# Two-part fp32 products: the high weights meet both halves of the operand in one 512-column matmul, in the FFN output and the last MLP

## The reference, cut to what matters

```
def swiglu(n, w_ffn_in, w_ffn_out):            # first block; its output projection is touched
    g, u = jnp.split(n @ w_ffn_in, 2, axis=-1)
    return (jax.nn.silu(g) * u) @ w_ffn_out     # 2816 -> 1024

def sq_relu_mlp(x, w_up, w_down):               # second block, layer 1 of 2 (the last MLP) is touched
    hdn = jax.nn.relu(x @ w_up)                 # 1024 -> 4096
    return (hdn * hdn) @ w_down                 # 4096 -> 1024

h = h + sq_relu_mlp(rms_norm(h, norm_mlp[i]), mlp_w_up[i], mlp_w_down[i])
```

## Time and profile before

| what | value |
|---|---|
| time, 3 runs | 1304.88, 1305.71, 1305.90 us; median 1305.71 |
| the profiled execution's own time | 1304.97 us |
| its span, first to last instruction | 1303.2 us (mean granted TensorE clock 0.985) |
| busy in the span | PE 1244.8 us (96%), DVE 862.6 us (66%), ACT 672.1 us (52%), POOL 36.5 us (3%) |
| chain that ended last | PE 85%, DVE 10%, ACT 3% of the span |

### The profile page before, as it was taken

The page is one execution under the profiler, slowest core; times in us unless marked ns, Lnnn a source line. Parts: engine busy times, 40 slices in busy tenths (PEclk is TensorE's granted clock), DMA queues, the critical chain, the costliest instruction groups (busy, mean ns, idle before and its releaser), DMA issues.

```text
span 1303.2 us, 26044 instructions
## 1 busy us (share of the span) xinstructions
PE 1244.8 (96%) x9778; PEld 1199.2 (92%) x9778; DVE 862.6 (66%) x1308; ACT 672.1 (52%) x1027; POOL 36.5 (3%) x58
## 2 busy tenths in 40 slices
PE   5989999999998999999799999999999988999997
PEld 5989779999997999999799879999999977999996
DVE  6897674888755877765754545766554869766543
ACT  6443435657444656644434454655444685666331
POOL 1001220200000000000100000000000000000000
PEclk9999999999999999999899999999999988999999
DMA  5455333475552566565354202555555435556651
GB/s 198 138 162 162 114 97 114 130 236 185 163 161 97 172 187 189 179 191 181 103 187 127 68 1 85 169 170 174 179 177 172 150 111 154 179 188 182 188 179 65
DMA packets 56759, 197.52 MB, mean 152 GB/s; under 512 B 7136, under 2 KB 9440, under 8 KB 56560
## 3 DMA queue, kind: packets, MB, share of 16 engines
q1 hardware_dynamic: 54144, 194.01, 48.0%
q10 hardware_dynamic: 2544, 2.51, 0.6%
HBM read 195.45 MB, written 1.05 MB: 151 GB/s over the span
## 4 chain that ended last, share of the span: by engine, by line
PE 85%; DVE 10%; ACT 3%; issue 2%; DMA 1%; SPq 0%; DVEq 0%; ACTq 0%
PE acc L392 23%; PE acc L394 23%; PE acc L393 23%; DVE wlo L1246 3%; PE acc L437 2%; PE acc L438 2%; PE acc L439 2%; ACT whi L863 1%; PE mix L521 1%; DVE xc L1450 1%; PE mix L734 1%; DVE uu L1735 1%; DMA raw<-w 1%; PE mix L695 1%; PE mix L744 1%
## 5 line engine op out<-in xcount | busy, mean ns | idle before, releaser
L863 ACT ACTIVATE whi<-raw 128x1024 fp32r<-128x1024 f32 x368 | 388.1, 1058 | 464.4 <-PE acc L394 405.4
L1246 DVE TENSOR_TENSOR wlo<-raw,whi 128x1024 fp32r<-128x1024 f32 x368 | 449.5, 1223 | 220.9 <-ACT whi L863 220.4
L392 PE MATMUL acc<-xh,whi 128*128 128x256 f32 (+1 forms) x1664 | 479.1, 288 | 24.0 <-DVE xl L1253 20.7
L394 PE MATMUL acc<-xh,wlo 128*128 128x256 f32 (+1 forms) x1664 | 474.7, 285 | 0.0
L393 PE MATMUL acc<-xl,whi 128*128 128x256 f32 (+1 forms) x1664 | 474.5, 285 | 0.0
L392 PEld LDWEIGHTS acc<-xh,whi 128*128 128x128 f32 x1664 | 317.4, 191 | 29.5 <-DVE wlo L1246 17.6
L394 PEld LDWEIGHTS acc<-xh,wlo 128*128 128x128 f32 x1664 | 318.0, 191 | 0.0
L393 PEld LDWEIGHTS acc<-xl,whi 128*128 128x128 f32 x1664 | 316.5, 190 | 0.2
L393 PE MATMUL acc<-hl,whi 128*128 128x256 f32 (+1 forms) x688 | 195.4, 284 | 0.0
L392 PE MATMUL acc<-hh,whi 128*128 128x256 f32 (+1 forms) x688 | 195.0, 283 | 0.0
L394 PE MATMUL acc<-hh,wlo 128*128 128x256 f32 (+1 forms) x688 | 194.7, 283 | 0.0
(11 more groups left out here) (322 smaller groups left out, 1478.3 us busy)
## 6 DMA issues: line engine op xcount, KB each, us to landing
raw<-w SPq DMA_DIRECT2D x368, 512.0 KB, 3.6
hT<-xT ACTq DMA_DIRECT2D x1, 1024.0 KB, 10.4
mem<-memT ACTq DMA_DIRECT2D x1, 1024.0 KB, 6.0
out<-hT SPq DMA_DIRECT2D x8, 128.0 KB, 2.0
xdt<-wsmall ACTq DMA_DIRECT2D x1, 192.0 KB, 10.2
pr<-par ACTq DMA_DIRECT2D x1, 114.0 KB, 10.1
hT<-metaT ACTq DMA_DIRECT2D x1, 64.0 KB, 11.5
bcn<-wa ACTq DMA_DIRECT2D x1, 32.0 KB, 10.1
```

The costliest lines, as they stand in the source:

```text
L392: nc.tensor.matmul(dst, whi[:, slot, n, :], rh, start=first, stop=False)
L394: return nc.tensor.matmul(dst, wlo[:, slot, n, :], rh, start=False, stop=last)
L863: act.activation(whi[:, j, :, :].rearrange("p k c -> p (k c)"), raw[:, j, :], ACT.Copy)\
L1246: dve.tensor_tensor(wlo[:, j, :, :].rearrange("p k c -> p (k c)"), raw[:, j, :], whi[:, j, :, :].rearrange("p k c -> p (k c)").bitcast(F32 ...
```

## The change

All three passes stay in the arithmetic, but the two that share `whi` become one instruction. The operand's high and low parts now lie side by side in one tile (`xboth`, `hboth`), and `wide` issues one matmul of 2 x 256 columns with `whi`, whose first half goes to columns 0 to 255 of the bank and whose second half to columns 256 to 511, and one of 256 columns with `wlo`, into the first half. The two halves of the bank are added up when the bank is read out. This is done for the 256-token phases `ffo`, `up1` and `dn1`; all other phases keep `products`.

```
-        xh = sb("xh", [P, KB, T2], F32R)
-        xl = sb("xl", [P, KB, T2], F32R)
+        xboth = sb("xboth", [P, KB, 2, T2], F32R)
+        xh, xl = xboth[:, :, 0, :], xboth[:, :, 1, :]
...
+        hboth = sb("hboth", [P, MLP_KB, 2, T2], F32R, stack=s3)
+        low = sb("low", [P, 4, T1], stack=s3)
+        hh, hl = hboth[:, :, 0, :], hboth[:, :, 1, :]
... TensorE
+            def wide(bank, slot, n, r, first, last):
+                nc.tensor.matmul(acc[:, bank, :].rearrange("p (a t) -> p a t", a=2), whi[:, slot, n, :], r, start=first,
+                                 stop=False, skip_group_check=True)
+                return nc.tensor.matmul(acc[:, bank, 0:T1], wlo[:, slot, n, :], r[:, 0, :], start=False, stop=last,
+                                        skip_group_check=True)
... ffo, DVE
-                    dve.tensor_tensor(h, acc[:, m % 4, 0:T1], h, ALU.add).then_inc(evacuated[m % 4], 1)
+                    dve.tensor_tensor(h, acc[:, m % 4, 0:T1], h, ALU.add).then_inc(joined, 1)
+                    dve.wait_ge(joined, m + 1)
+                    dve.tensor_tensor(h, acc[:, m % 4, T1:2 * T1], h, ALU.add).then_inc(evacuated[m % 4], 1)
```

```
+            def relu_squared(i, j):                                    # ACT, body of units_loop("up1")
+                act.wait_ge(unit_done, 4 * i + (UNITS["up1"][0] + j + 1))
+                act.activation(low[:, j, :], acc[:, j, T1:2 * T1], ACT.Copy).then_inc(low_ready, 1)
+                act.wait_ge(hid_ready, 4 * i + (2 * FFN_KB + MLP_KB + j + 1))
+                act.activation(blk(hh, 4 * i + j, 0, T1), t4[:, j, 0:T1], ACT.Copy).then_inc(hh_ready, 1)
... DVE, after inverse_rms("mlp1", T1)
-            units_loop("up1", *mlp_up(1, T1))
+            dve.tensor_tensor(rstdh[:, 0:T1], rstd[:, 0:T1], rstd[:, 0:T1], ALU.mult).then_inc(rstdh_ready, 1)
+            dve.wait_ge(rstdh_ready, 2)
+            def hid_sum(i, j):                                         # before split_lo of the unit four ahead
+                t = t4[:, j, 0:T1]
+                dve.wait_ge(low_ready, 4 * i + j + 1)
+                dve.wait_ge(hl_ready, 4 * i + (FFN_KB + MLP_KB + j - 3))
+                dve.tensor_tensor(t, acc[:, j, 0:T1], low[:, j, :], ALU.add).then_inc(evacuated[j], 1)
+            def hid_square(i, j):                                      # after it
+                t = t4[:, j, 0:T1]
+                dve.wait_ge(evacuated[j], i + (OUTS["up1"] // 4 + 1))
+                dve.scalar_tensor_tensor(out=t, in0=t, scalar=0.0, in1=t, op0=ALU.max, op1=ALU.mult)\
+                    .then_inc(hid_ready, 1)
+            units_loop("up1", hid_sum, hid_square)
... dn1, DVE, for each of 8 outputs
-                        dve.tensor_tensor(h, acc[:, m % 4, 0:T1], h, ALU.add).then_inc(evacuated[m % 4], 1)
+                        dve.tensor_tensor(t, acc[:, m % 4, 0:T1], rstdh[:, 0:T1], ALU.mult).then_inc(scaled_done, 1)
+                        dve.tensor_tensor(v, acc[:, m % 4, T1:2 * T1], rstdh[:, 0:T1], ALU.mult)\
+                            .then_inc(evacuated[m % 4], 1)
+                        dve.wait_ge(scaled_done, 2 * m + 1)
+                        dve.tensor_tensor(h, t, h, ALU.add).then_inc(scaled_done, 1)
+                        dve.wait_ge(evacuated[m % 4], (OUTS["dn1"] + m) // 4 + 1)
+                        dve.wait_ge(scaled_done, 2 * m + 2)
+                        dve.tensor_tensor(h, v, h, ALU.add).then_inc(joined, 1)
... POOL
+            with pool.Fori(0, MLP_KB // 4) as i:
+                for j in range(4):
+                    b = 4 * i + j
+                    pool.wait_ge(hh_ready, 4 * i + (FFN_KB + MLP_KB + j + 1))
+                    pool.tensor_tensor(blk(hl, b, 0, T1), t4[:, j, 0:T1], blk(hh, b, 0, T1).bitcast(F32), ALU.subtract)\
+                        .then_inc(hl_ready, 1)
```

More of the change, by code:

```diff
@@ L230, in blocks_kernel @@
         s3 = ExitStack()
-        hh = sb("hh", [P, MLP_KB, T2], F32R, stack=s3)
-        hl = sb("hl", [P, MLP_KB, T2], F32R, stack=s3)
+        hboth = sb("hboth", [P, MLP_KB, 2, T2], F32R, stack=s3)
+        low = sb("low", [P, 4, T1], stack=s3)
+        hh, hl = hboth[:, :, 0, :], hboth[:, :, 1, :]
         s3.close()
@@ L287, in blocks_kernel @@
         sm_step, pv_done = sem("sm_step"), sem("pv_done")
+        low_ready, sum_done, scaled_done = sem("low_ready"), sem("sum_done"), sem("scaled_done")
+        joined = sem("joined")
         hid_ready, hh_ready, hl_ready = sem("hid_ready"), sem("hh_ready"), sem("hl_ready")
@@ L394, in products, with wide_unit @@
                 return nc.tensor.matmul(dst, wlo[:, slot, n, :], rh, start=False, stop=last)
+            def wide(bank, slot, n, r, first, last):
[3 more added lines that the diff above has]
+                                        skip_group_check=True)
+            def wide_unit(phase, m, j, turn=None, ready=None):
+                u0, e0 = UNITS[phase][0], OUTS[phase]
+                pe.wait_ge(lo_ready, m + (u0 + 1))
+                pe.wait_ge(evacuated[j], (e0 + m) // 4 if turn is None else turn + e0 // 4)
+                for k in range(KB):
+                    if ready is not None:
+                        pe.wait_ge(ready[0], ready[1] + k + 1)
+                    last = wide(j, (u0 + j) % 4, k, xboth[:, k, :, 0:T1], k == 0, k == KB - 1)
+                last.then_inc(unit_done, 1)
             def unit(phase, m, j, ah, al, T, turn=None, ready=None):
@@ L710, in ffn_down @@
                         pe.wait_ge(hl_ready, k + 1)
-                    last = products(acc[:, m % 4, 0:T1], (u0 + b // 8) % 4, b % 8, hh[:, k, 0:T1], hl[:, k, 0:T1],
-                                    k == 0, k == FFN_KB - 1)
+                    last = wide(m % 4, (u0 + b // 8) % 4, b % 8, hboth[:, k, :, 0:T1], k == 0, k == FFN_KB - 1)
                     if b % 8 == 7:
@@ L787, in mlp @@
             def mlp(n, T):
-                project(f"up{n}", xh, xl, T, operand(f"mlp{n}"),
-                        statistics=lambda: stream_stats(f"mlp{n}", T))
+                if T == T1:
+                    for j in range(4):
+                        wide_unit(f"up{n}", j, j, ready=operand(f"mlp{n}") if j == 0 else None)
+                        if j == 0:
+                            stream_stats(f"mlp{n}", T)
+                    with pe.Fori(1, MLP_KB // 4) as i:
+                        for j in range(4):
+                            wide_unit(f"up{n}", 4 * i + j, j, turn=i)
+                else:
+                    project(f"up{n}", xh, xl, T, operand(f"mlp{n}"),
+                            statistics=lambda: stream_stats(f"mlp{n}", T))
                 with pe.Fori(0, 2) as i:
@@ L803, in deep4 @@
                         pe.wait_ge(hl_ready, hid0 + k + 1)
-                    last = products(acc[:, m, 0:T], (u0 + k // 8) % 4, k % 8, hh[:, k, 0:T], hl[:, k, 0:T],
-                                    k == 0, k == MLP_KB - 1)
+                    if T == T1:
+                        last = wide(m, (u0 + k // 8) % 4, k % 8, hboth[:, k, :, 0:T1], k == 0, k == MLP_KB - 1)
+                    else:
+                        last = products(acc[:, m, 0:T], (u0 + k // 8) % 4, k % 8, hh[:, k, 0:T], hl[:, k, 0:T],
+                                        k == 0, k == MLP_KB - 1)
                     if k % 8 == 7:
@@ L1229, in _ @@
             rms("mlp1", T1, (), 8)
-            units_loop("up1", mlp_up(1, T1))
+            def relu_squared(i, j):
[3 more added lines that the diff above has]
+                act.activation(blk(hh, 4 * i + j, 0, T1), t4[:, j, 0:T1], ACT.Copy).then_inc(hh_ready, 1)
+            units_loop("up1", relu_squared)
             u0 = UNITS["dn1"][0]
@@ L1235, in _ @@
                         split_hi(u0 + 4 * m + n + 4)
-                act.wait_ge(evacuated[m % 4], (OUTS["dn1"] + m) // 4 + 1)
+                act.wait_ge(joined, KB + m + 1)
                 square(m, T1)
@@ L1843, in _ @@
                     if n == 3:
-                        h = hT[:, m, META:T2]
-                        dve.tensor_tensor(h, acc[:, m % 4, 0:T1], h, ALU.add).then_inc(evacuated[m % 4], 1)
+                        h, t, v = hT[:, m, META:T2], t4[:, m % 4, 0:T1], low[:, m % 4, :]
+                        dve.tensor_tensor(t, acc[:, m % 4, 0:T1], rstdh[:, 0:T1], ALU.mult).then_inc(scaled_done, 1)
[6 more added lines that the diff above has]
+                        dve.tensor_tensor(h, v, h, ALU.add).then_inc(joined, 1)
                     if u0 + 4 * m + n + 4 < NU:
```

## The result

The changed kernel takes 1331.4 us (median of 6 runs, 1330.22 to 1333.44) where the kernel before takes 1305.8 (6 runs). The ratio is 1.0203, with a 95% interval of 1.0192 to 1.0214. Forecast were 1327.0 us and a range of 1320 to 1338. The profiled execution took 1330.22 us, its span is 1328.5 us, 25.3 more than before.

A forecast was written before the change was run, and what follows sets the result against it. PE was taken to bound all three phases before the change, ACT and DVE's closed order up1 after it. -2.1 + 24.6 + 0.4 - 2.7 + 1.1 = +21.3 us took 1304.97 to 1326.3, median 1327.0; range 1320 to 1338.

The forecast's parts named there:

- up to the root of up1's norm (ffo): In ffo, 176 blocks each save 11.8 ns by the 512-column pass: -2.1 us.
- up1 until the fourth unit of dn1: PE waits in each up1 unit once the four buffered units are used up, beginning dn1's fourth unit 24.6 us late.
- the rest of dn1: In dn1, one leftover wait costs +0.4 us and the other 29 units gain -2.7 us.
- the end: After the last output of dn1, DVE has four instructions instead of one before ACT's square: 1.56 us instead of 0.42, +1.1.
- The ring: In up1, ACT and DVE steps wait for each other in a closed order: 3.76 us per unit against PE's 2.75.
- The wide pass: In ffo, up1 and dn1, a 512-column pass replaces two of 256: a block costs 343.7 ns instead of 355.5.
- I take 225: A 512-column pass takes 225 ns, its fixed 11.8 ns paid once, against 237 if paid for each half.
- pays its fixed part twice: Rival, 7%: the 512-column pass pays its fixed part for each half, ffo and dn1 give back 4.8 us: 1331.8.
- The sustained rate: Rival, 2%: 512-column passes at about 131 ns save 106 ns a block in ffo and dn1, up1 wait kept: 1288.5.
- The clock: Rival, 4%: PE's clock falls because it waits about 1.0 us in each up1 unit; at 0.65, 1341.
- POOL: Rival, 5%: POOL's subtraction meets DVE in every up1 unit, 0.48 us each time, +14.4 us: 1341.4.
- PE's fifth unit of dn1: In dn1, one wait is left over from up1's last hh copy, split_hi and split_lo: +0.4 us.

The follow-up runs named there:

- the ring shortened: The changed kernel with DVE's relu-square in up1 right after the sum, before split_lo instead of behind it: 1303.9 us, ratio 1.0001.
- the ring opened: The changed kernel with ACT in up1 copying the previous unit's result into hh, the last of each four at once: 1306.0 us, ratio 1.0009.
- the ring closed in the kernel before: The kernel before, three 256-column passes, with only DVE's relu in up1 moved behind split_lo: 1323.9 us, ratio 1.0153.
- The sweep: The changed kernel with another pass shape for each of ffo's eight outputs, 128 to 512 columns: 117.8 ns at 256 columns, 234.5 at 512.
- the sweeps: Two changed kernels with other pass shapes for each ffo output, the second also with bf16 and narrow weights: 512 columns 234.5 ns in fp32r, 215 in bf16.

## Why the prediction was right, and where its sizes were off

The profiled execution was forecast at +21.3 us and came out at +25.3. By steps:

| step | forecast | measured | from |
|---|---|---|---|
| up to the root of up1's norm (ffo) | -2.1 | -1.3 | ACT's root at 1111.82, before 1113.13 |
| up1 until the fourth unit of dn1 | +24.6 | +25.7 | 122.2 us from that root (to 1233.98), before 96.4 (to 1209.54) |
| the rest of dn1 | -2.3 | -0.3 | 82.7 us to the last read-out, before 83.0 |
| the end | +1.1 | +1.2 | 1.65 us to the square, before 0.46 |

All four steps came out later than forecast, so none of these errors hid another.

**The ring, right.** Each of its steps is in the profile, with each wait where it was foretold. It came out at 3.81 us against 3.76. One step was mis-sized: from the end of low to the sum are 0.12 us (1148.54 to 1148.66), not the 0.03 that the reciprocal's start suggested. Low and split_hi are 0.05 shorter together than their rows of before, the last two steps 0.01 each, and the loop's end adds 0.02 on average. 30 turns make 1.4 us of the 0.05, of which an earlier start gives 0.3 back. Three experiments show the cause from three sides: the ring shortened, the ring opened, and the ring closed in the kernel before.

**The wide pass, wrong in size.** The term that was mis-sized comes from "I take 225". It rests on the reading that 11.8 ns come once for each pass, drawn from two passes only 16 columns apart. The sweep shows the price from 256 columns on to be near 1.5 ns and 0.455 ns for each column: 118 at 256, 234 at 512. A block of dn1 saves 3.3 ns, not 11.8: a unit takes 2.827 us (1243.17 to 1251.65, three releases of ACT's split_hi by PE) where it took 2.854 (1209.80 to 1292.58, 29 units), and in the sweep 3 x 117.8 less 350 is 3.4. The dn1 step had counted 2.7 us for its 29 units; 0.8 are there, and that 1.9 is the largest part of the miss. In ffo the same price gives 0.6 us in place of 2.1; the other 0.7 of its row in the table lie elsewhere up to there, and where was not looked for. The rival that named this ("pays its fixed part twice") had the nearer price, 237 for a measured 234, for a wrong reason: two runs cost no more than one. That its 1331.8 lies 0.4 us from the median is luck, since it gave the blocks no gain at all and left the ring at 3.76.

**The sustained rate** of 131 ns at 512 columns, of the Trainium skill's page "TensorE: Matmul & The Clock Gate", section "Back-to-back issue gap", was given 2%. The trace disagrees: in the sweeps passes of 512 columns follow each other after 215 ns (bf16) and 234 ns (fp32r).

**The clock** stayed at 1.00 with PE waiting in each unit, as the window of 73% busy had it. **POOL** took 0.74 us each time. It started some 0.2 us after ACT's copy, not 0.08, and still ended before the sum, as was worked out from the earlier trace rows (1148.27 and 1148.66); the ring did not pay for it. **PE's fifth unit of dn1** waited 0.35 us for the split left over from the ring, 0.4 forecast.

**The end** took the four instructions' time as foretold, 1316.69 to 1318.34:

```profile
1316.69 0.42 DVE L1907 TENSOR_TENSOR t<-acc,rstdh 128x256 f32<-128x256 f32 x1 [8.31 <-PE acc L409]
1317.04 0.41 DVE L1908 TENSOR_TENSOR low<-acc,rstdh 128x256 f32<-128x256 f32 x1
1317.37 0.41 DVE L1911 TENSOR_TENSOR hT<-t,hT 128x256 f32<-128x256 f32 x1
1317.88 0.42 DVE L1914 TENSOR_TENSOR hT<-low,hT 128x256 f32<-128x256 f32 x1
...
1318.34 0.42 ACT L905 ACTIVATE sq<-hT 128x256 f32<-128x256 f32 x1 [10.98 <-DVE hT L1914]
```

## What to carry to other kernels

When a change adds a handoff between two engines that run in program order, write one unit of both programs as a circle and add up the steps from each wait to the next: if the circle closes within the unit, no unit takes less than its sum, however idle both engines look, and a ring of buffers hides it only until what it had in store is used up (here eight units). It is enough to make the sum no longer than what the bottleneck engine needs, by an instruction that comes earlier, or to open the circle in one place, by work that lags a unit. And before merging passes to save what each costs once, measure that cost on sizes far apart; 256 and 272 columns could not tell a fixed part from a higher price for each column.

## What the runs showed of the hardware that was not expected

- From 256 to 512 columns an fp32r column costs 0.455 ns of pass spacing at a granted clock of 1.00, a bf16 column 0.42 (512 columns: 234 and 215 ns); at 384 columns fp32r is 3 ns below that line.
- An fp32r pass with 128 columns of weights is followed after about 112 ns on average, with 128 columns of operand and with 192; with 64 columns of weights 60 ns were reached, and in bf16 with 128 columns of both 56 ns.
- A DVE instruction and a POOL instruction, both on SBUF, hold each other up: where they meet, the square takes 0.97 us instead of 0.42, and POOL's subtraction 1.31 instead of 0.74. The Trainium skill, page "SBUF — State Buffer", section "SBUF: two separate sides", says so of a DVE instruction with two SBUF inputs, and the numbers agree.
